# Two extra 64-row matmuls behind three spreads, and activations moved by 32 bytes in SBUF

## What is computed

```python
for l in range(DEPTH):                       # DEPTH = 2, SEQ = 256, D_MODEL = 1024, D_FF = 2816
    x = x + 0.5 * swiglu(rmsnorm(x, ffn1_norm[l]), ffn1_w_gate[l], ffn1_w_up[l], ffn1_w_down[l])
    x = x + hybrid_mixer(rmsnorm(x, mix_norm[l]), w_in[l], ...)
    x = x + 0.5 * swiglu(rmsnorm(x, ffn2_norm[l]), ffn2_w_gate[l], ffn2_w_up[l], ffn2_w_down[l])
return rmsnorm(x, final_norm)
# swiglu(x) = (silu(x @ w_gate) * (x @ w_up)) @ w_down
```

## Time and profile before

| | |
|---|---|
| time, median of 3 runs | 925.46 us |
| the profiled execution | 924.28 us, span 922.5 us |
| TensorE matmuls (PE) | busy 914.4 us, 99% |
| TensorE weight loads (PEld) | 907.6 us, 98% |
| VectorE (DVE) | 606.2 us, 66% |
| ScalarE (ACT) | 455.7 us, 49% |
| HBM read | 167.55 MB, 183 GB/s over the span |

### The profile page before, as it was taken

How to read it: one execution, slowest core, us unless ns; L and a number is a source line. 1 busy time by engine, 2 the same in 40 slices (tenths; PEclk the granted TensorE clock), 3 DMA queues, 4 the chain that set the end, 5 groups by cost and what they waited for, 6 DMA issues and landing times.

```text
span 922.5 us, 19279 instructions
## 1 busy us (share of the span) xinstructions
PE 914.4 (99%) x8100; PEld 907.6 (98%) x8100; DVE 606.2 (66%) x723; ACT 455.7 (49%) x527; POOL 3.5 (0%) x7
## 2 busy tenths in 40 slices
PE   9999999999999999999999999999999999999997
PEld 9999999999999999999999999999999999999996
DVE  7755565688768665555685555567797685565554
ACT  7544443468756444444554444445685644444443
POOL 0000000000000000000000000000000000000001
PEclk9999999999999999999999999999999999999999
DMA  8765665664356655655556665665623676655631
GB/s 285 243 225 182 201 204 186 185 181 120 90 169 220 223 187 183 199 191 200 182 186 212 192 194 182 198 209 142 211 65 92 228 229 189 215 188 183 197 121 46
DMA packets 131191, 169.16 MB, mean 183 GB/s; under 512 B 3440, under 2 KB 116944, under 8 KB 131152
## 3 DMA queue, kind: packets, MB, share of 16 engines
q1 hardware_dynamic: 130576, 167.96, 57.2%
q10 hardware_dynamic: 576, 0.66, 0.2%
HBM read 167.55 MB, written 1.05 MB: 183 GB/s over the span
## 4 chain that ended last, share of the span: by engine, by line
PE 97%; DMA 1%; DVE 0%; SPq 0%; ACT 0%; POOL 0%; POOLq 0%; issue 0%
PE ps L401 31%; PE ps L403 30%; PE ps L402 30%; PE ps L673 1%; PE ps L660 1%; DMA resid<-in_xt 1%; PE ps L522 1%; PE ps L530 0%; PE ps L538 0%; PE ps L793 0%; PE ps L495 0%; PE ps L489 0%; PE ps L755 0%; PE ps L732 0%; PE ps L481 0%; PE ps L775 0%
## 5 line engine op out<-in xcount | busy, mean ns | idle before, releaser
L1153 DVE TENSOR_TENSOR wlo<-raw,whi 128x2048 fp32r<-128x2048 f32 x157 | 351.2, 2238 | 234.2 <-ACT whi L880 234.1
L401 PE MATMUL ps<-xhi,whi 128*128 128x256 f32 x1584 | 438.7, 277 | 0.0
L402 PE MATMUL ps<-xlo,whi 128*128 128x256 f32 x1584 | 437.3, 276 | 0.0
L403 PE MATMUL ps<-xhi,wlo 128*128 128x256 f32 x1584 | 437.3, 276 | 0.0
L880 ACT ACTIVATE whi<-raw 128x2048 fp32r<-128x2048 f32 x157 | 294.1, 1873 | 129.1 <-PE ps L403 128.6
L401 PEld LDWEIGHTS ps<-xhi,whi 128*128 128x128 f32 x1584 | 297.4, 188 | 0.6
L403 PEld LDWEIGHTS ps<-xhi,wlo 128*128 128x128 f32 x1584 | 297.4, 188 | 0.0
L402 PEld LDWEIGHTS ps<-xlo,whi 128*128 128x128 f32 x1584 | 297.4, 188 | 0.0
L401 PE MATMUL ps<-h_parts,whi 128*128 128x256 f32 x768 | 212.3, 276 | 0.0
L402 PE MATMUL ps<-h_parts,whi 128*128 128x256 f32 x768 | 212.2, 276 | 0.0
L403 PE MATMUL ps<-h_parts,wlo 128*128 128x256 f32 x768 | 212.1, 276 | 0.0
(11 more groups left out here) (173 smaller groups left out, 544.4 us busy)
## 6 DMA issues: line engine op xcount, KB each, us to landing
raw<-in_ffn_w_down SPq DMA_DIRECT2D x44, 1024.0 KB, 4.9
raw<-in_ffn_w_gate SPq DMA_DIRECT2D x42, 1024.0 KB, 5.4
raw<-in_ffn_w_up SPq DMA_DIRECT2D x42, 1024.0 KB, 5.4
raw<-in_w_in SPq DMA_DIRECT2D x12, 1024.0 KB, 5.2
raw<-in_w_in SPq DMA_DIRECT2D x8, 512.0 KB, 4.5
raw<-in_w_out SPq DMA_DIRECT2D x8, 512.0 KB, 4.7
raw<-in_w_in SPq DMA_DIRECT2D x2, 1088.0 KB, 5.2
raw<-in_w_out SPq DMA_DIRECT2D x8, 256.0 KB, 3.7
```

The source lines that it names most:

```text
L401: pe.matmul(o, w_hi, x_hi, start=start, stop=False, skip_group_check=True)
L402: pe.matmul(o, w_hi, x_lo, start=False, stop=False, skip_group_check=True)
L403: return pe.matmul(o, w_lo, x_hi, start=False, stop=stop, skip_group_check=True)
L1153: nc.vector.tensor_tensor(lo, r, h.bitcast(F32), ALU.subtract).then_inc(lo_done, 1)
```

## The change

The unused tensor in front of `xhi` shrinks from 96 to 88 floats. Everything declared behind it moves by 32 bytes: `x` from 448 to 416 bytes modulo 512, `h_parts` from 192 to 160, and also `sq`, `par`, `cst`, `work` and all of the mixer's tensors. The weights and `resid` stay. In `ffn`, a call of `half_rows(1)` follows the spread of the three later FFN norms.

```diff
-        sb("gap_x", [P, 96])
+        sb("gap_x", [P, 88])
         xhi = sb("xhi", [P, KT, SEQ], F32R)
@@
                     split_ready(2, t)
                     up_tile(tiles(0)[:, 0, :], 2, 0)
                     spread_r(5 * l + 4 * f, rs_y)
+                    half_rows(1)
                     up_tile(tiles(0)[:, 1, :], 2, 1).then_inc(unit_done, 1)
                     up(0, t + 1, 1)
```

## The result

The changed kernel takes 955.7 us (median of four, 955.33 to 956.25), against 924.98 us for the kernel before: ratio 1.0336, 95% interval 1.0324 to 1.0348. The forecast was 927.9 us, and the range ended at 935.0 us.

What follows compares the result with a forecast made beforehand. TensorE was taken as the bound: matmul count times distance between starts, plus breaks. 924.28 us plus 2.5 us for half_rows, nothing for the move, gave 926.8 us profiled, 927.9 us as median; range 916.5 to 935.0 us.

Steps and rivals of the forecast that it cites:

- The half_rows cost 3 x 0.82 = 2.5 us: Behind the three later FFN norms' spreads, each half_rows adds 0.82 us to TensorE's path, with nothing hiding it.
- Nothing taken for the move: The 32-byte move was priced at zero, since x at 448 and h_parts at 192 bytes ran at the same 113.3 ns.
- The bound upward: All 7056 matmuls over x or h_parts running 4.5 ns slower, at 117.9 ns each: 32 us more.
- the short pace: 113.3 ns from start to start of 256-column matmuls, seen in the long FFN stretches of the kernel before.
- Rival 3: An FFN runs 4.5 ns slower per matmul throughout, 6.7 us each: 934.6 us for one, 948 for three; chance 0.15.
- the long pace: About 117.9 ns between matmul starts, 4.5 ns over the short pace, seen in the output projection and other stretches outside FFN loops.
- Its two remarks: Output projection falls into the long pace without a break; nothing interrupts an FFN loop, so the long pace would stay.
- Rival 2: The pace itself falls toward the 111.9 ns of line 793's matmuls, up to 9.9 us less, down to 918.0 us; chance 0.32.
- Rival 1: The loose stretches lock into the short pace, saving 2.1 us: 925.8 us; chance 0.12.
- the loose stretches: Matmul runs outside the FFN loops (first units, output projection, mixer products) whose pace might change: 2.1 us less or 2.3 more.
- The port rule: TensorE's moving operand and weight loads have independent read ports, so distance can't matter and the change costs only 2.5 us.
- signs of being wrong: FFN count in 196 us (1731 unchanged, 1752 at 111.9 ns, 1663 at 117.9) moving by five, or mixer breaks growing or vanishing.

Runs made afterwards that it cites:

- half_only: Only the three new half_rows added to the kernel before, without the 32-byte move: 927.25 us against 924.76 us.
- plus_256: Kernel before with x and h_parts 256 bytes further from the weights (192 and 448 bytes modulo 512): 924.6 us, ratio 1.000.
- sweep: Kernel before, then 26 unread streams of 42 matmuls at shifted distances, other engines idle: 113.3 ns at 192 and 448, 117.4 at 160 and 416.
- move_only: Only the 32-byte move made to the kernel before, without the three new half_rows: 961.2 us, ratio 1.038.
- h_only: Kernel before with only h_parts moved, to 160 bytes modulo 512, x kept at 448, no new half_rows: 954.6 us.
- before_bare: Kernel before without the half_rows that it executes in four places: 928.5, 943.7, 949.8 and 950.6 us in four executions.
- sweep_rows: Kernel before, then 64 unread streams in 4-byte steps of distance, each directly behind two 64-row matmuls: 113.3 ns at best, no total time given.
- sweep_direct: The same 64 streams behind the kernel before, each entered from 18 matmuls at distance 192; of these entries 44 ran at 113.3 ns, 20 at 117.8.

## Why the prediction was wrong, point by point

- **TensorE's pace times its matmuls is the bound: right.** In every kernel of the study the time follows the distance between starts, and no wait of TensorE is longer than 1.2 us.
- **The half_rows cost 3 x 0.82 = 2.5 us: right**, 2.5 us measured alone (`half_only`).
- **Nothing taken for the move: the step that failed.** Its argument was that 448 and 192 bytes give the same pace, so that part must be flat. They are the same point: the period is 256 bytes (`plus_256`, `sweep`). One point had been seen, not two, and the curve on both sides of it is 3 to 10 ns higher. The move costs 28 us with the half_rows (955.7 - 927.3) and 36 us without.
- **The bound upward was in the text, 32 us, and was left out of the range.** The reason given was that the short pace follows the half_rows wherever they stand. That held for one distance only, and there in four places of the one trace; in the streams it failed in 20 of 64. At 160 bytes no short pace was seen to lead back to. Behind the spread the changed kernel has 117.3 ns in all three FFNs, where `move_only` has 120.0, 118.7 and 120.0; behind the output projection's transposes it has 118.8 ns in spite of half_rows (the window from 272 us). All in all the new ones are worth 961.2 - 955.7 = 5.5 us net, far less than the loss.
- **Rival 3, an FFN at the long pace:** nearest to the truth in kind, but its price was set for one to three FFNs and it got 0.15. All four were slow, and the mixer too, since the cause is the distance and not a missed return. Its two remarks were sound: `h_only` shows an unmoved stream kept long by the one before it, and `before_bare` shows what happens where nothing ends the long pace.
- **Rival 2, a lower pace:** no distance in steps of 4 bytes gives less than 113.3 ns. The 111.9 ns of line 793 is another kind of stream and bounded nothing here.
- **Rival 1, the loose stretches:** they went the other way. The stretch of the earlier trace rows takes 5.64 us after, as good as before, but `M_R1` in front of it takes 5.86 us in place of 5.55 us.
- **The port rule:** with all other engines idle, the streams took 113.3 to 123.5 ns by the place of the moving operand alone (`sweep_rows`, `sweep_direct`). By the Trainium skill's page "SBUF — State Buffer", section "Who interferes with whom", the two reads of TensorE are independent; then the distance couldn't matter, and the measurement decides against that as far as time goes. Why the distance matters was not shown: no run looked inside.
- **Two slips in the signs of being wrong.** Five matmuls in 196 us are 0.33 ns each, 2.3 us in all: a little less than the half_rows' 2.5 us, not more. And 1752 and 1663 leave out the two matmuls begun before the stretch, which 1731 has. Neither touches the forecast.

## What to carry to other kernels

Where TensorE is the bound, the pace from start to start deserves a look of its own, and so does the distance between the moving and the stationary operand in SBUF: here it was worth up to 9% of a matmul's time, and the right point was 4 bytes wide. Two equal values of a curve say little until its period is known, and a bound that the rows give should stay in the range unless a row of the new condition, not of the old one, excludes it. A distance that comes back to its best pace from every entry seen (112 here) is worth more than one that extra instructions lead back most of the time, even if both have the same best pace. And a table of single looks is weak where a pace is partly a matter of chance: the same entry has to be repeated.

## What the runs showed of the hardware that I had not expected

- The pace of float32r matmuls (128x128 stationary weights, 256 columns of `x` moving) repeats with 256 bytes of distance between the two operands, and is sharp: 113.3 ns at 112 and 192, 116.5 to 123.5 ns at the other 62 multiples of 4 (two looks at each). Where weights moved over `x` in the kernels, the pace was another than in the streams at the same distance: 113.3 ns against 117.8 at 64, 120 ns against 116.6 at 144.
- Many distances have more than one steady pace: 113.3 and 117.8 ns at 192; 117.3, 118.7 and 120.0 ns at 160; 117.4 and 120.0 ns at 8. The choice falls at a break or a change of stream, and it can last for a whole FFN of 170 us. The same two 64-row matmuls in front gave the short pace at 192 in 44 of 64 entries.
- At 192, executions of one and the same program differ by 22 us without half_rows (three of four were long), and with them most agree within 2 us, but 7 of 42 took 6 to 20 us more.
